# Expert pairs of a two-layer decoder: the gather moved into the down products, a form of three groups and one, another order of pairs and phases

## The reference

```python
def moe_swiglu(h, w_router, b_router, w_gate, w_up, w_down):
    ...
    probs = jax.nn.softmax(logits, axis=-1)
    top_p, top_e = lax.top_k(probs, TOP_K)
    top_p = top_p / jnp.sum(top_p, axis=-1, keepdims=True)
    ...
    def expert_block(args):
        xb, e = args
        return swiglu(xb, w_gate[e], w_up[e], w_down[e])
    ...
    out = jnp.zeros((T + 1, d), jnp.float32).at[slot_tok].add(ys.astype(jnp.float32) * slot_p[:, None])

def swiglu(h, w_gate, w_up, w_down):
    return (jax.nn.silu(h @ w_gate) * (h @ w_up)) @ w_down
```

## Time and profile before

| what | us |
|---|---|
| median of three runs | 1342.48 |
| the profiled execution | 1343.16 |
| its span | 1341.3 |
| PE busy in the span | 1277.4 (95%) |
| DVE, ACT, POOL busy | 219.8, 124.5, 36.1 |
| mean granted clock | 0.988 |

### The profile page before, as it was taken

How to read it: one execution, slowest core, us unless ns; L and a number is a source line. 1 busy time by engine, 2 the same in 40 slices (tenths; PEclk the granted TensorE clock), 3 DMA queues, 4 the chain that set the end, 5 groups by cost and what they waited for, 6 DMA issues and landing times.

```text
span 1341.3 us, 28791 instructions
## 1 busy us (share of the span) xinstructions
PE 1277.4 (95%) x12903; PEld 746.0 (56%) x12904; DVE 219.8 (16%) x597; ACT 124.5 (9%) x247; POOL 36.1 (3%) x125
## 2 busy tenths in 40 slices
PE   7999999999998699999899999999999999999995
PEld 3777788877885433346565534665343555343553
DVE  0299200000005601010110201002010002010002
ACT  2201310000002310000001000001000001000002
POOL 1000100000003200000000000000000000000000
PEclk9899999999999899999999999999999999999998
DMA  9999575556436299999999899999999999999993
GB/s 334 408 402 387 202 277 201 211 174 231 162 121 251 90 406 417 418 420 423 420 407 352 356 365 423 392 381 420 417 418 420 422 419 417 419 418 418 423 419 121
DMA packets 87885, 462.23 MB, mean 345 GB/s; under 512 B 8747, under 2 KB 12119, under 8 KB 52663
## 3 DMA queue, kind: packets, MB, share of 16 engines
q1 hardware_dynamic: 85937, 456.41, 85.1%
q10 hardware_dynamic: 1814, 3.85, 0.8%
HBM read 458.94 MB, written 2.24 MB: 344 GB/s over the span
## 4 chain that ended last, share of the span: by engine, by line
PE 80%; DMA 13%; DVE 2%; issue 2%; POOL 1%; ACT 1%; SPq 0%; DVEq 0%; ACTq 0%; POOLq 0%
PE bank L1624 36%; PE bank L1389 25%; DMA ring<-in_w_exp_down_dram 13%; PE bank L1646 9%; PE bank L1572 2%; PE bank L1358 2%; PE bank L1678 1%; PE bank L1595 1%; PE bank L1286 1%; POOL ROWS L625 1%; SPq L527 0%; DVE xT L957 0%; ACT MIX L890 0%; PE bank L1516 0%; PE bank L1337 0%
## 5 line engine op out<-in xcount | busy, mean ns | idle before, releaser
L1624 PE MATMUL bank<-ring,HT 128*32 128x512 f32 (+1 forms) x5376 | 510.1, 539 | 3.5 <-DMA ring<-in_w_exp_up_dram 3.5
L1624 PEld LDWEIGHTS bank<-ring,HT 128*32 128x32 f32 x5376 | 189.1, 110 | 312.5 <-issue 298.2
L1389 PE MATMUL bank<-HT,ring 128*128 128x264 f32 x1024 | 234.0, 390 | 2.5 <-POOL HT L619 2.5
L1389 PEld LDWEIGHTS bank<-HT,ring 128*128 128x128 f32 x1024 | 195.4, 192 | 43.6 <-issue 10.3
L1646 PE MATMUL bank<-ring,hid_t 128*32 128x256 f32 x2560 | 149.2, 379 | 2.6 <-DMA ring<-in_w_exp_down_dram 2.6
L1646 PEld LDWEIGHTS bank<-ring,hid_t 128*32 128x32 f32 x2560 | 86.2, 110 | 56.3 <-issue 5.6
L1389 PE MATMUL bank<-BIG,ring 128*128 128x264 f32 x480 | 107.3, 386 | 0.0
L1389 PEld LDWEIGHTS bank<-BIG,ring 128*128 128x128 f32 x480 | 91.1, 190 | 15.5
L1646 PE MATMUL bank<-ring,COND 128*32 128x256 f32 x1568 | 89.6, 380 | 9.9 <-DMA ring<-in_w_exp_down_dram 9.7
L1646 PEld LDWEIGHTS bank<-ring,COND 128*32 128x32 f32 x1568 | 50.2, 110 | 47.8 <-DMA ring<-in_w_exp_down_dram 18.5
L1223 DVE TENSOR_TENSOR hid_t<-bank,hid_t 128x512 f32<-128x512 f32 (+1 forms) x22 | 14.2, 643 | 361.0 <-PE bank L1624 360.3
(11 more groups left out here) (230 smaller groups left out, 527.8 us busy)
## 6 DMA issues: line engine op xcount, KB each, us to landing
ring<-in_w_exp_gate_dram SPq DMA_DIRECT2D x64, 1024.0 KB, 15.1
ring<-in_w_exp_up_dram SPq DMA_DIRECT2D x64, 1024.0 KB, 16.2
ring<-in_w_exp_down_dram SPq DMA_DIRECT2D x64, 1024.0 KB, 24.1
ring<-in_w_ada_dram SPq DMA_DIRECT2D x48, 1024.0 KB, 12.9
ring<-in_w_exp_gate_dram SPq DMA_DIRECT2D x64, 768.0 KB, 16.0
ring<-in_w_exp_up_dram SPq DMA_DIRECT2D x64, 768.0 KB, 14.6
ring<-in_w_exp_down_dram SPq DMA_DIRECT2D x32, 1536.0 KB, 25.2
ring<-in_w_in_dram SPq DMA_DIRECT2D x10, 1024.0 KB, 24.9
```

The source lines that it names most:

```text
L1389: ins = t_.matmul(banks_of[label][:, 0:NT], w[:, k, f * P:(f + 1) * P], src(k0 + k), start=(k0 + k == 0), stop=(k0 + k == k_tiles - 1))
L1624: ins = t_.matmul(bank[GATE_BANKS[role][g]][i * GRP:(i + 1) * GRP, 0:cols], xg[:, k, c0:c0 + GRP], w[:, i, :], start=(k == 0), stop=(k == ...
```

## The change

`RANK_AT` makes the pairs 88 with 17, 149 with 16, 85 with 54 and 83 with 36 tokens, and a fourth form `thin` runs three groups and one: 4, 6, 5 and 5 groups. The phases are written out (`STEPS`): for the first part large gate, large up, small gate, small up; the second part is large gate, small gate, large up, small up; down as before. As the first 16 loads are now all of expert 0 (`KNOWN`), SP waits for the flags at the seventeenth; the first 14 loads wait each for the unit that held their room, and nothing else.

The gather of pair p+1 stands in pair p's down phases, in four pieces of six matmuls, in banks 3 to 6 and always 224 columns wide; the last pair gathers too. Pair 0's gather stands ahead of the loop and of the wait for the flags, and on DVE its pick matrices stand ahead of the flags' work. ACT copies the next pair's batch behind the Silus of this one. The store and spread of the tables move from ACT to POOL.

```diff
-VARIANTS = (("narrow", (3, 2)), ("slim", (5, 1)), ("mid", (5, 2)))
-SLIM = 2
-RANK_AT = (0, 4, 1, 7, 2, 5, 3, 6)
+VARIANTS = (("narrow", (3, 2)), ("slim", (5, 1)), ("thin", (3, 1)), ("mid", (5, 2)))
+THIN, SLIM = 0, 2
+RANK_AT = (0, 6, 1, 7, 2, 4, 3, 5)
...
+STEPS = (("large", "gate", 0), ("large", "up", 0), ("small", "gate", 0), ("small", "up", 0),
+         ("large", "gate", 1), ("small", "gate", 1), ("large", "up", 1), ("small", "up", 1),
+         ("large", "down", 0), ("small", "down", 0), ("large", "down", 1), ("small", "down", 1))
+PHASES = tuple((role, kind, HALVES[role][f]) for role, kind, f in STEPS)
+KNOWN = 2 * DT
...
-GATHER_BANKS = (0, 1, 2, 3)
+GATHER_BANKS = (3, 4, 5, 6)
...
-                    if first and n == DT:
+                    if first and n == KNOWN:
...
-                    if (role, kind, i) != ("small", "gate0", 0):
+                    if first and n < RING:
+                        sp.wait_ge(ring_used, UNITS0 - RING + n + 1)
+                    elif (role, kind, i) != ("small", "gate0", 0):
                         sp.wait_ge(ring_used, base + (UNITS0 + loads_before(end)))
...
+            pool.wait_ge(on("pmT_ready"), 1)
+            pool.dma_start(pm_rows, pmT[:]).then_inc(on("pm_rows_stored"), 16)
+            pool.wait_ge(on("pm_rows_stored"), 16)
+            for i, dst in enumerate((posb, wgtb)):
+                spread = pm_rows[i * NE:(i + 1) * NE, :].rearrange("e n -> (e n)").unsqueeze(0)
+                pool.dma_start(dst.rearrange("p e n -> p (e n)"),
+                               spread.to_broadcast([P, NE * NT])).then_inc(on("tables_spread"), 16)
...
             def pair_scalar(p, j, groups):
-                take_batch(p, groups)
...
+                take_batch(p + 1)
                 act.wait_ge(on("large_out_done"), p + 1)
...
+            pe.wait_ge(on("pick_ready"), 1)
             for bk in range(7):
                 pe.wait_ge(emptied[bk], bank_total[bk])
+            for i in range(len(GATHER_BANKS)):
+                gather(0, i)
             pe.wait_ge(on("flags_ready"), 1)
...
                         for turned in turns.get(u, ()):
                             turn_hid(*turned)
+                        if u in gathers:
+                            gather(p + 1, gathers[u])
...
-                gather(p, groups)
...
+                turns = {("small", "up", 0): {0: large[0][:3], 3: large[0][3:]},
+                         ("large", "gate", 1): {3: small[0]},
+                         ("small", "up", 1): {early: large[1][:3], late: large[1][3:]},
+                         ("large", "down", 0): {4: small[1]}}
+                gathers = {("large", 0): {1: 0, 2: 1}, ("small", 0): {8: 2, 10: 3}}
```

More of the change, by code:

```diff
@@ L449, in each_pair @@
             with nc.body(f"{tag}_not_slim", valid_engines=[kind]):
+                eng.br_eq(form, THIN, on_true=f"{tag}_thin", on_false=f"{tag}_not_thin")
+            with nc.body(f"{tag}_not_thin", valid_engines=[kind]):
                 eng.br_lt(form, SLIM, on_true=f"{tag}_narrow", on_false=f"{tag}_mid")
@@ L835, in _, with take_batch @@
             rows(2)
[L838 to L844, removed]
+            def take_batch(p):
+                for i, b in enumerate(GATHER_BANKS):
+                    act.wait_ge(on("gathered"), p * 4 + (i + 1))
+                    src = bank[b][:, 0:2 * BOTH].rearrange("p (t n) -> p t n", t=2)
+                    a.activation(xg[:, 2 * i:2 * i + 2, :], src, ACT.Copy).then_inc(on("xg_ready"), 1)
             def pair_scalar(p, j, groups):
-                take_batch(p, groups)
                 for s in range(2):
@@ L1553, in _, with gather @@
             fill("turned", ins)
+            ring_flat = ring[:].rearrange("p s n -> p (s n)")
+            L, S = MOST["large"], MOST["small"]
+            def gather(p, i):
+                b = GATHER_BANKS[i]
+                for half in range(2):
+                    d = 2 * i + half
+                    for t in range(3):
+                        ins = t_.matmul(bank[b][:, half * BOTH:(half + 1) * BOTH], h_rows[:, t, d * P:(d + 1) * P],
+                                        pick[t], start=(half == 0 and t == 0), stop=(t == 2), skip_group_check=True)
+                ins.then_inc(on("gathered"), 1)
+            pe.wait_ge(on("pick_ready"), 1)
             for bk in range(7):
                 pe.wait_ge(emptied[bk], bank_total[bk])
+            for i in range(len(GATHER_BANKS)):
+                gather(0, i)
             pe.wait_ge(on("flags_ready"), 1)
@@ L1558, in _ @@
             pe.wait_ge(emptied[7], bank_total[7])
[L1560 to L1568, removed]
-                    for i in range(2):
-                        d = 2 * b + i
-                        for t in range(3):
-                            ins = t_.matmul(bank[b][:, i * BOTH + lo:i * BOTH + hi], h_rows[:, t, d * P:(d + 1) * P],
-                                            pick[t][:, lo:hi], start=(i == 0 and t == 0), stop=(t == 2), skip_group_check=True)
-                    ins.then_inc(on("gathered"), 1)
             def pair_tensor(p, j, groups):
@@ L1653, in down @@
                         ins.then_inc(on(f"{role}_out_done"), 1)
-                gather(p, groups)
                 early, late = (4, 7) if count["small"] == 1 else (3, 5)
-                for s in range(2):
-                    large = [("large", s, g) for g in range(count["large"])]
-                    before_it = [("small", s - 1, g) for g in range(count["small"])] if s else []
-                    expand("large", "gate", s, {3: before_it})
-                    expand("small", "gate", s, {})
-                    expand("large", "up", s, {})
-                    expand("small", "up", s, {early: large[:3], late: large[3:]})
-                down("large", 0, {4: [("small", 1, g) for g in range(count["small"])]})
-                down("small", 0, {})
-                down("large", 1, {})
-                down("small", 1, {})
+                large, small = ([[(role, s, g) for g in range(count[role])] for s in range(2)] for role in ROLES)
+                turns = {("small", "up", 0): {0: large[0][:3], 3: large[0][3:]},
[3 more added lines that the diff above has]
+                gathers = {("large", 0): {1: 0, 2: 1}, ("small", 0): {8: 2, 10: 3}}
+                for role, kind, s in STEPS:
+                    if kind == "down":
+                        if (role, s) == ("large", 0):
+                            pe.wait_ge(on("pick_ready"), p + 2)
+                        down(role, s, turns.get((role, kind, s), {}), gathers.get((role, s), {}))
+                    else:
+                        expand(role, kind, s, turns.get((role, kind, s), {}))
+                pe.wait_ge(on("xg_ready"), p * 4 + 8)
                 pe.wait_ge(on("place_ready"), p * GMAX + GMAX)
```

48 lines of the change are left out of this document (20 added, 28 removed).

## The result

The changed kernel took 1355.24 us (median of 4 runs, 1353.65 to 1357.78) beside 1342.57 for before: ratio 1.0096, 95% interval 1.0073 to 1.0119. Repeated among the experiments, it gave 1354.63, 1.0096 [1.0079, 1.0113]. The forecast was 1343.1, no change; the changed kernel is 12 us above that. The profiled execution of after took 1357.78 (span 1356.0).

A forecast was written before the change was run, and what follows sets the result against it. The end was taken to follow how early the weights' queue gets going and how early PE reaches pair 1's last phase. Terms -1.1 - 9.2 + 9.6 + 1.3 = +0.6 us, stated against the median: 1343.1 us, range 1337.5 to 1347.5.

The forecast's parts named there:

- The fourth form adds a branch to the issue time; nothing.: Entry to the forms: the added form thin costs one more branch of issue time, put at nothing.
- Boundary, -9.2: Pair 0's last landing to pair 1's first expert matmul: shorter tail and scatter, no gather, less clock terms; -9.2 us.
- The gather for pair 2, +9.6: Pair 1's down phase, where PE counts: four added gather pieces cost +9.6 us, bounds 9.5 to 10.3.
- The last pair, +1.3: Last pair's down phases: a gather for no pair, mostly absorbed, costs +1.3 us, between 0 and 2.7.
- Start, -1.1: Entry and first weight loads: the queue gains 2.1 us, less 1.0 for a lower clock; -1.1 us.
- The queue from the load at 899.86 on: From pair 2's fifth load, the last to wait for room, to 1319.2: the queue never stops for long.
- The dropped group: Pair 0 loses a group, hidden by the queue; only half of 1.93 us and scatter 3.76 for 4.70 show.
- Up behind gate: New phase order, up following gate: the Silu waits are covered, cost nothing; uncovered 0.9 us.
- Half clock out of pair 0: Rival at pair 0's end: at 1.2 GHz tail and scatter take 9.4 us, +4.5, 1347.0 us; chance 0.20.
- Faster, with the clock up: Rival at entry and boundary: gaps drop no clock, so -3.7, 1338.8 us; chance 0.27.
- The queue is all: Rival at the start: only bytes count, six loads earlier are 15 us, 1327.5 us; chance 0.03.
- doesn't do what it says: Rival in pair 0: it still runs two small groups, PE passes the queue, 1352 us; chance 0.03.

The follow-up runs named there:

- the layout alone put right: Changed kernel with its forms laid out narrow, thin, slim, mid instead of narrow, slim, thin, mid: 1348.41 us, 1.0038 of before.
- the run with the hint: Changed kernel laid out narrow, thin, slim, mid, with a PE branch hint for the jump to thin ahead of the first gather: 1347.44 us.
- the run with the small gather: Changed kernel laid out narrow, thin, slim, mid, the form of pairs 2 and 3 gathering one tile of three: 1346.19 us.
- thin, slim, narrow, mid: Changed kernel with its four forms laid out in this order, so both jumps ahead of pairs 0 and 1 go: 1348.57 us, 1.0036 of before.
- the two layouts of before's kernel with the new pairs: Kernel before with only the new pairs and form thin: narrow, thin, slim, mid 1340.92 us, repeated 1340.03; thin, slim, narrow, mid 1342.60 us.
- the one that broke it: Kernel before with the new pairs, laid out thin, slim, mid, narrow, so the jump ahead of pair 2 goes over a body: 1355.86 us.
- the run with the new pairs alone: Kernel before with only the new pairs and form thin, laid out narrow, thin, slim, mid: 1340.92 us, 0.9978 of before; repeated 1340.03.

## Why the prediction was wrong

**The step that failed** is one half sentence: "The fourth form adds a branch to the issue time; nothing." The branch itself is nothing (0.08 us). Its target is: the form of pair 0 changed, and with it which code lies behind it. At the boundary the jump took 6.3 to 6.6 us where 0.3 stood. With the layout alone put right, the time falls by 6 to 8 of the 12 us.

**Boundary, -9.2.** Of this, 1.7 is half clock on pair 1's first matmuls, which the table books in pair 1; for the boundary's own column the forecast is -10.9. **Measured: -4.3** (14.7 for 19.0), 6.6 short. From the scatter's end to the first expert matmul PE stood idle for 7.0 us, where I had 2.6; with a short jump it was 0.9, so the jump cost 6.1, and my 2.6 was 1.7 too much. **The half clock was mis-sized as well:** tail and scatter took 7.7 us in both profiles of after, for the 4.71 of my sum, so 3.0 where I had put 0.8. With full clock, in the run with the hint, they took 4.9. Together: 6.1 - 1.7 + 2.2. With the layout right the column was 7.3, as my sum without its clock terms gives, but that is luck: 1.7 us more in tail and scatter, 1.7 less behind them. Three other profiles of that layout gave 5.8, 6.7 and 8.3.

**The gather for pair 2, +9.6: right by itself.** Its pieces take 2.47 us, four of them 9.9, and the run with the small gather has 10.2. With the 1.7 of half clock named above, the forecast for pair 1's column is +11.3; it grew by 12.5 to 12.7. In after the rest is the half clock on its first matmuls, 678.93 to 685.76 (the first two rows are for the paragraphs on the rivals and the start):

```profile
665.28:672.11 6.83, 5.82 (x52) 3.85 (x56) 0.03 (x1) 1.67 (x2) 0.00 (x0) 0.50 1.01 422
474.13:480.96 6.83, 4.45 (x24) 1.18 (x28) 2.84 (x10) 1.28 (x1) 0.00 (x0) 0.50 0.03 7
678.93:685.76 6.83, 4.76 (x24) 1.23 (x28) 3.01 (x11) 0.00 (x0) 0.00 (x0) 0.50 1.01 417
```

4.76 us of matmuls at 1.2 GHz instead of 2.4 are an estimated 2.4 lost, where I had 1.7. PE had been idle for 7.07 us ahead of them. With slim behind thin the clock stays up there, but 1.9 us of fetch come in its place; with thin, slim, narrow, mid it is 3.5 of fetch and 3.4 at half clock behind it. For the fetch the sum had no term: I priced what moved in and the clock, and not what else the moved piece had covered where it was.

**The last pair, +1.3: measured +2.4**, within the bounds given (0 to 2.7), near the upper. The chain's last piece of down products is 34.67 us long without a landing in it: PE had fallen behind the queue.

**Start, -1.1: measured +1.9 and +0.7** at pair 0's last landing, counted from the sorted tables' product, which by itself came 1.4 us later in after's profile than in before's. The first gather began 2.16 us behind it (forecast 2.3) and took 10.85 us (11.7). Then came the jump: the first expert matmul stood 17.8 us behind the product instead of 16.9. The fifteenth load was issued 5.8 us behind that matmul (at 482.35) where I had 3.7, with PE at half clock from 474.13 to 480.96, and landed 4.9 us later (5). Without the jump, in the layout thin, slim, narrow, mid, the start comes out at -4.0. But, as the two layouts of before's kernel with the new pairs show, little of it would have reached the end.

**The queue from the load at 899.86 on** was right: 419.3 in before, 419.0 to 419.8 in twelve other profiles, whatever came before; the one that broke it gives the rule its bound. **The dropped group** costs nothing, and with the gather where it was it brings 1.7 and 2.9 us. **Up behind gate**: nothing, as said. **Rest**: 0.5 and 1.1 us more at the end than before, not foreseen and not explained.

**The rivals.** None named the jump. Half clock out of pair 0 came true in part: 665.28 to 672.11 stood at 0.50, and tail and scatter took 7.7 us, between the 4.7 of my sum and the 9.4 of that rival. That is some 3 of the 12 us. It doesn't make a kernel slow by itself: in the run with the new pairs alone, 664.53 to 671.36 stood at 0.50, tail and scatter took 7.9 us, and that kernel is faster than before. Faster, with the clock up: not seen. "The queue is all" and "doesn't do what it says": not so.

The sum, put right from the two profiles of after: start +1.3, boundary -4.3, pair 1 +12.6, tail +2.4, queue +0.1, rest +0.8, together +12.9 for the 12.0 to 12.7 measured. Against the +0.6 of the forecast 12.3 us are missing: 6.6 at the boundary, 2.4 at the start, 1.3 in pair 1, 1.1 in the tail, 0.9 in queue and rest.

## What to carry to other kernels

Where code is chosen at run time, the order of the bodies in memory is part of the schedule: put behind each body the one that follows it on the path that counts, and look at the taken jumps whenever a new variant or order of data makes another body run first. Before moving work out of a place, ask what it covers there besides what it waits for: long matmuls with few instructions hide the fetch of the code behind them. A change in several parts should be run by its parts; here one part alone (the pairs) gained 2 to 3 us, and all of them together lost 12.

## What the hardware showed that I had not expected

- A jump into a form over a body on PE lasted 3.9 to 7.5 us (15 jumps without a hint), with one or two packets of 16,384 bytes of instructions in it; 0.25 to 0.44 us into the body directly behind the one just run. One jump with three packets lasted 10.79.
- It needs no crowded queue. At the entry of after and two of its variants the weights' queue stood still and the jump took 3.9 to 5.1 us; with weights moving it was 5.7 to 7.5.
- When the head of the next body is there but not its next block, PE ran 31 to 60 matmuls and then waited 1.4 to 3.5 us (five profiles).
- The jump back to the loop's head, with its hint at the start of each body, took 0.36 to 4.1 us. Behind pair 2 it was 1.8 to 4.1 in eleven profiles and 0.4 in the three with thin laid out first. A hint ahead of the forward jump brought that one to 2.84 in the one profile of it.
